# Block inverse of an RWKV-7 scan: every second head's 64x64 products cross to the other half of the partitions

## The chip, the cores and the metric

The kernel runs on one core of a Trainium2 chip. The metric is the device time of one execution in microseconds (us), as the median of several. The engines are TensorE (PE in the profile, its weight loads PEld), VectorE (DVE), ScalarE (ACT), GpSimd (POOL) and SyncE (SP), which here only issues DMAs. Each has its own program and meets the others at semaphores.

## What is computed

One layer of a hybrid block on 2048 tokens of width 1024: RMSNorm, an input projection, a mixer of two groups (8 RWKV-7 heads of width 64 and a spatial gate), an output projection, cross-attention to 256 memory tokens, and a SwiGLU network. The change is in the RWKV-7 heads. Cut to that:

```python
def wkv7_scan(r, w, k, v, kk, a):
    def step(S, inp):
        r_t, w_t, k_t, v_t, kk_t, a_t = inp
        sa = jnp.einsum('bhvk,bhk->bhv', S, -kk_t)
        S = (S * w_t[:, :, None, :]
             + sa[..., None] * (kk_t * a_t)[:, :, None, :]
             + v_t[..., None] * k_t[:, :, None, :])
        y = jnp.einsum('bhvk,bhk->bhv', S, r_t)
        return S, y
```

The kernel does not step through the tokens. It takes them in chunks of 64, where `sa` of a chunk is the solution of a triangular system. So each head and chunk needs the inverse of a unit triangular 64x64 matrix.

## The kernel before

The stage of the heads comes after the input projection and before the output projection. It goes over 16 groups of 128 tokens (`GROUPS`). One group holds 16 triangular matrices: head pair `m` (0 to 3), head `e` of the pair (0 or 1), and `a` (0 or 1), which says on which half of the partitions the matrix lies (`lane(a)`: partitions 0 to 63 or 64 to 127) and which chunk of 64 tokens it is. The inverse `inv` has the shape [128, e, m, 64].

It is built by doubling. It starts as the identity with 2x2 blocks put in (`take_first`), and five levels (`LEVELS` = 2, 4, 8, 16, 32) join neighbouring blocks. A level has these steps, each on another engine than the one before it:

1. PE, `cross` (L1942): 16 products of `inv_t` (the transposed inverse) with the scores `atrb`, 32 columns each, into PSUM.
2. ACT, `evac_x` (L1220): copies PSUM into `xm`.
3. PE, `merge` (L1953): 16 products of `xm` with `inv`, again 32 columns each.
4. DVE, `take_level` (L2551, in the helper `take`): puts the result into `inv` under a mask.
5. DVE, `turned` (L2566): transposes `inv` into `inv_t` for the next level.

Every level is cut in two by the parity `g` of the head pair. The half `g` = 0 goes to bank 0 and `g` = 1 to bank 1, and each half has its own semaphore count at every step. So `cross` of `g` = 1 may run while ACT copies `g` = 0. All 16 products read one half of the partitions and write the same half (`unit(a, g, ...)` from `lane(a)`): of the array's four 64x64 tiles (row half, column half) they use the two on the diagonal.

Each engine has one hand-written order of work, `body`, which mixes three groups: the state and outputs of group k (`state_...`), the inverse and scores of group b = k + 1, and the preparation of group n = k + 2. The order on PE in one body, with the inverse in capitals: from_values, state_out 0, state_in 0, scores of `bt`, solve 0, scores of `kt`, state_add 0, chunk_out 0, CROSS 0, state_out 1, state_in 1, MERGE 0, mix_gate, solve 1, CROSS 1, state_add 1, turn_gate, MERGE 1, chunk_out 1, turn kt, loras, CROSS 2, key_norms, variance, bonus_sums, MERGE 2, lora_g, CROSS 3, turn_v, MERGE 3, key_scales, scale_back, turn bt, CROSS 4, MERGE 4. `turn bt` transposes `bt` into PSUM; ACT copies that into `b_tok`. `solve` of the next body needs the finished inverse.

ACT in one body: identities, rhs_t 0, sa_t 0, inputs, xm 0, rhs_t 1, sa_t 1, xm 1, outputs, k_tok, `lora_tanh` (L1244, tile `th`), xm 2, `roots` (L1252, after a load of the function table), `deviation`, `exps` (after a second load), xm 3, gate, v_tok, b_tok, xm 4.

DVE in one body: take_first, transposes 0, scores into `atrb`, next_state 0 (writes `h_st`, L2593), scores into `qkrm`, take 0, transposes 1, mixed, next_state 1, take 1, transposes 2, gate statistics, `sum_decays` (waits for `th`), `bounded` (waits for ACT's roots), take 2, transposes 3, two reciprocals, `gate_hat`, `bonuses`, take 3, transposes 4, keys_normed, normalised, queries, decayed (writes `bt` of the group after), take 4.

## Time and profile before

| what | us |
|---|---|
| median of 3 runs | 2953.13 (2949.37 to 2953.44) |
| the profiled execution's own time | 2955.44 |
| its span, first to last instruction | 2953.6 |
| the stage of the 16 groups in it, about | 594 to 1040 |

The profile comes from one execution. A row of the grouped views gives a line of the kernel, the engine, what is written and read, shapes and count, then the busy time, the mean of one instruction in ns, and the idle time just before it with what ended it. A row of the timeline gives the start in us, the length in us, engine, line, operation, tiles and count; several like instructions are merged into one row, whose length runs from the first start to the last end. A product of fp32 operands makes two PE records, so 16 products are x32. Instructions in one queue overlap a little: the second of two copies starts before the first has ended.

### The profile page before, as it was taken

The numbers are of one execution on the slowest core, as the hardware profiler recorded it, in microseconds if no ns is written. First come the engines' busy times: TensorE is split into PE (matmuls) and PEld (weight loads), VectorE is DVE, ScalarE is ACT, GpSimd is POOL, SyncE is SP. The second block draws the span as 40 slices with busy tenths as digits, with TensorE's granted clock in tenths as the row PEclk, the third lists the DMA queues.
The fourth block names the chain that finished last, engine by engine and source line by source line (L and its number), as shares of the span: only waits on it lengthen the run. The fifth ranks groups of instructions, "written<-read, shape, count | busy, mean of one in ns | idle before, by whom it ended". The sixth has DMA issues, their size and how long they took to land.

```text
span 2953.6 us, 56334 instructions
## 1 busy us (share of the span) xinstructions
PE 2894.0 (98%) x23722; PEld 2461.5 (83%) x23722; DVE 1590.1 (54%) x2062; ACT 1000.5 (34%) x1740; POOL 1484.9 (50%) x1070
## 2 busy tenths in 40 slices
PE   8999999999999999999999999999999999999998
PEld 7888888888888879987888888787998788888887
DVE  7331633377777632339666644544234966674453
ACT  4122312244554522325333322231333433332222
POOL 4554543456666544276544433556426654553344
PEclk9999999999999999999999999999999999999999
DMA  4533356422232231112333356344111223336632
GB/s 159 186 111 97 122 164 191 148 67 53 57 79 68 66 104 37 51 50 84 111 128 142 122 214 236 134 143 157 43 44 43 100 111 125 142 121 228 228 143 86
DMA packets 175572, 346.56 MB, mean 117 GB/s; under 512 B 46816, under 2 KB 104352, under 8 KB 169696
## 3 DMA queue, kind: packets, MB, share of 16 engines
q1 hardware_dynamic: 175328, 343.06, 34.2%
q8 instruction: 184, 3.01, 0.4%
q14 instruction: 60, 0.49, 0.1%
HBM read 240.24 MB, written 102.76 MB: 116 GB/s over the span
## 4 chain that ended last, share of the span: by engine, by line
PE 48%; DVE 3%; issue 1%; DMA 1%; POOL 1%; ACT 0%; DVEq 0%; SPq 0%; ACTq 0%; POOLq 0%
PE ps L2259 29%; PE ps L1697 14%; PE ps L2211 3%; DMA w_raw<-in_weights 1%; DVE normed L3185 0%; DVE t_raw L2879 0%; POOL sumsq L853 0%; PE ps L2417 0%; DVE t_raw L2887 0%; POOL sq L851 0%; DVE rstd L2429 0%; PE ps L2231 0%; DVE t_lo L2893 0%; POOL w_lo L833 0%; DVE normed L3211 0%
## 5 line engine op out<-in xcount | busy, mean ns | idle before, releaser
L833 POOL TENSOR_TENSOR w_lo<-w_raw,w_hi 128x512 fp32r<-128x512 f32 x232 | 334.9, 1467 | 504.3 <-ACT w_hi L1138 500.6
L1697 PE MATMUL ps<-a_hi,w_hi 128*128 128x512 f32 x1140 | 446.0, 391 | 10.5 <-DVE a_lo L2439 10.0
L1697 PE MATMUL ps<-a_lo,w_hi 128*128 128x512 f32 x1140 | 444.7, 390 | 0.0
L1697 PE MATMUL ps<-a_hi,w_lo 128*128 128x512 f32 x1140 | 351.8, 390 | 0.0
L1138 ACT ACTIVATE w_hi<-w_raw 128x512 fp32r<-128x512 f32 x228 | 129.9, 623 | 623.9 <-PE ps L1697 481.4
L2259 PE MATMUL ps<-a_hi,w_hi 128*128 128x512 f32 x800 | 313.8, 392 | 12.5 <-ACT p_t L1524 4.9
L2259 PE MATMUL ps<-a_lo,w_hi 128*128 128x512 f32 x800 | 312.4, 390 | 0.0
L2259 PE MATMUL ps<-a_hi,w_lo 128*128 128x512 f32 x800 | 312.3, 390 | 0.0
L1697 PEld LDWEIGHTS ps<-a_hi,w_hi 128*128 128x128 f32 x1140 | 214.6, 188 | 55.4 <-DVE a_lo L2439 10.0
L1697 PEld LDWEIGHTS ps<-a_hi,w_lo 128*128 128x128 f32 x1140 | 214.6, 188 | 44.8
L1697 PEld LDWEIGHTS ps<-a_lo,w_hi 128*128 128x128 f32 x1140 | 214.7, 188 | 44.1 <-issue 0.2
L1064 POOL TENSOR_TENSOR w_lo<-w_raw,w_hi 128x512 fp32r<-128x512 f32 x100 | 143.2, 1432 | 182.7 <-ACT w_hi L1508 182.7
L1064 POOL TENSOR_TENSOR w_lo<-s,w_hi 128x512 fp32r<-128x512 f32 x100 | 146.0, 1460 | 163.1 <-ACT w_hi L1508 163.1
L2801 DVE TENSOR_TENSOR x<-ps,x 128x1024 f32 (+1 forms) x63 | 76.7, 1222 | 267.9 <-PE ps L1697 255.2
L2447 DVE TENSOR_TENSOR z_ext<-ps,rstd 128x1024 f32<-128x1024 f32 x44 | 53.9, 1226 | 304.7 <-PE ps L1697 304.2
L1697 PE MATMUL ps<-b_hi,w_hi 128*128 128x512 f32 x512 | 202.3, 395 | 3.7 <-DVE x L2801 3.7
L1697 PE MATMUL ps<-b_lo,w_hi 128*128 128x512 f32 x512 | 200.9, 392 | 0.0
L1064 POOL TENSOR_TENSOR xw_lo<-s,xw_hi 128x512 fp32r<-128x512 f32 x100 | 145.1, 1455 | 110.7 <-ACT xw_hi L1508 110.7
L2259 PE MATMUL ps<-t_hi,xw_hi 128*128 128x512 f32 x496 | 193.5, 390 | 1.3 <-DVE u_t L2949 1.1
L2259 PE MATMUL ps<-t_lo,xw_hi 128*128 128x512 f32 x496 | 193.2, 389 | 0.0
L2259 PE MATMUL ps<-t_hi,xw_lo 128*128 128x512 f32 x496 | 193.0, 389 | 0.0
L2259 PEld LDWEIGHTS ps<-a_hi,w_hi 128*128 128x128 f32 x800 | 150.7, 188 | 47.8 <-ACT p_t L1524 6.6
(381 smaller groups left out, 6392.0 us busy)
## 6 DMA issues: line engine op xcount, KB each, us to landing
w_raw<-in_weights SPq DMA_DIRECT2D x228, 512.0 KB, 4.1
hidden<-hid SPq DMA_DIRECT2D x44, 1024.0 KB, 3.9
zT<-z_out SPq DMA_DIRECT2D x44, 512.0 KB, 3.4
a_hi<-hidden SPq DMA_DIRECT2D x44, 512.0 KB, 8.4
a_lo<-hidden SPq DMA_DIRECT2D x44, 512.0 KB, 9.6
w_raw<-kvw SPq DMA_DIRECT2D x32, 512.0 KB, 3.3
suv<-zT SPq DMA_DIRECT2D x16, 512.0 KB, 4.5
x<-in_xT SPq DMA_DIRECT2D x16, 512.0 KB, 5.7
```

Source lines behind the costliest of these rows:

```text
L833: pool.tensor_tensor(low_t[:, part, :], w_raw[:, u, part, :], high[:, part, :].bitcast(F32), ALU.subtract).then_inc(S["w_lo_done"], 1)
L1064: pool.tensor_tensor(operand(o, p)[1], operand_raw[o], operand(o, p)[0].bitcast(F32), ALU.subtract).then_inc(S["sw_lo"], 1)
L1138: act.activation(split_into(pair, u)[0][:, part, :], w_raw[:, u, part, :], ACT.Copy).then_inc(S["w_hi_done"], 1)
L1697: mm = pe.matmul(to[:, nb, 0:w], wt[:, k, :], r[:, k, nb * w:(nb + 1) * w], start=(k == 0 and r is hi_in and wt is high), stop=(k == kn - ...
L2211: mm = pe.matmul(to, st[:, k, at:at + P], wt[:, 0:2, k, :], start=(k == 0 and n == 0 and t % 2 == 0), stop=(k == KT - 1 and n == 2), skip_ ...
L2259: mm = pe.matmul(to, wt[:, k, :], r[:, k, :], start=(k == 0 and n == 0 and not more), stop=(k == HT - 1 and n == 2), skip_group_check=True)
L2447: dve.tensor_tensor(z_ext[:, u, 1:TB + 1], flat(src), rstd[:], ALU.mult).then_inc(S["job_out"], 1)
L2801: dve.tensor_tensor(at_k(x, k), flat(slot(beside + u)).unsqueeze(1), at_k(x, k), ALU.add).then_inc(S["job_out"], 1)
```

## The change

The cut by parity of the pair (`g`) is replaced by a cut by `e`. Matrices with `e` = 0 go as before. Products of `e` = 1 write the other half of the partitions (`unit(a ^ e, e, ...)`), so `cross` and `merge` now use all four 64x64 tiles. The results of `e` = 1 are thereby on the wrong half, and ACT (`evac_x`) and DVE (`take_level`) bring them back with two copies over 64 partitions each, in place of one over 128. Both waits of `cross` become one wait for both transposes, and both waits of `merge` one wait for all three copies. `xm` is laid out by `e` first, and the transposes read contiguous columns. On PE, `turn bt` goes from before `cross` 4 to between `cross` 4 and `merge` 4.

```diff
-                for g in range(2):
-                    act.wait_ge(S["x_ps"], 10 * n + 2 * lv + g + 1)
-                    act.activation(xm[:, :, g].rearrange("p e m (n two b) -> p e (m n) two b", two=2, b=b)[:, :, :, 0, :],
-                                   ps[:, g, 2 * L:3 * L].rearrange("p (e n b) -> p e n b", e=2, b=b), ACT.Copy).then_inc(S["x_ev"], 1)
+                for e in range(2):
+                    act.wait_ge(S["x_ps"], 10 * n + 2 * lv + e + 1)
+                    for to, frm in crossed(e):
+                        act.activation(sides(xm, e, to, b)[:, :, 0, :], blocks_in(e, 2 * L, frm, b), ACT.Copy).then_inc(S["x_ev"], 1)
...
+        def crossed(e):
+
+            if e == 0:
+                return ((slice(0, P), slice(0, P)),)
+            return ((lane(0), lane(1)), (lane(1), lane(0)))
...
-                for g in range(2):
-                    pe.wait_ge(S["inv_tr"], 10 * n + 2 * lv + g + 1)
-                    for mh, e, a in by_tile():
-                        t_u = inv_t[lane(a), g, 2 * e + mh, :].rearrange("p (n two b) -> p n two b", two=2, b=b)[:, :, 0, :]
-                        mm = pe.matmul(unit(a, g, 2 * L + e * C + mh * 32, 32), atrb[par][lane(a), e, 2 * mh + g, 0, :], t_u,
-                                       start=True, stop=True)
-                    mm.then_inc(S["x_ps"], 1)
+                pe.wait_ge(S["inv_tr"], 10 * n + 2 * lv + 2)
+                for m, e, a in by_tile():
+                    t_u = inv_t[lane(a), e, m, :].rearrange("p (n two b) -> p n two b", two=2, b=b)[:, :, 0, :]
+                    mm = pe.matmul(unit(a ^ e, e, 2 * L + m * 32, 32), atrb[par][lane(a), e, m, 0, :], t_u, start=True, stop=True)
+                    if (m, a) == (HP - 1, 1):
+                        mm.then_inc(S["x_ps"], 1)
...
-                for g in range(2):
-                    pe.wait_ge(S["x_ev"], 10 * n + 2 * lv + g + 1)
...
+                pe.wait_ge(S["x_ev"], 15 * n + 3 * lv + 3)
+                for m, e, a in by_tile():
+                    u_u = inv[par][lane(a), e, m, :].rearrange("p (n two b) -> p n two b", two=2, b=b)[:, :, 1, :]
+                    mm = pe.matmul(unit(a ^ e, e, m * 32, 32), xm[lane(a), e, m, :], u_u, start=True, stop=True)
+                    if (m, a) == (HP - 1, 1):
+                        mm.then_inc(S["tu_ps"], 1)
...
                 if behind:
+                    cross(b, q, 4)
                     turn(b, bt, "bt_done", (S["sg_vh"], min(b + 2, GROUPS)), 3, "btr")
-                    cross(b, q, 4)
                     merge(b, q, 4)
...
-                    dve.wait_ge(S["tu_ev"], 11 * n + (2 * lv + g if lv else 1))
-                    dve.transpose(inv_t[:, g], units(inv[par], g)).then_inc(S["inv_tr"], 1)
+                for e in range(2):
+                    dve.wait_ge(S["tu_ev"], 16 * n + ((3 * lv - 1, 3 * lv + 1)[e] if lv else 1))
+                    dve.transpose(inv_t[:, e], inv[par][:, e]).then_inc(S["inv_tr"], 1)
...
-                for g in range(2):
-                    dve.wait_ge(S["tu_ps"], 10 * n + 2 * lv + g + 1)
-                    take(rights(inv[par], g, b), low[:, lv + 1, 1].rearrange("p (m n b) -> p m n b", m=HP, b=b),
-                         ps[:, g, 0:2 * C].rearrange("p (m n b) -> p m n b", m=HP, b=b), "tu_ev")
+                for e in range(2):
+                    dve.wait_ge(S["tu_ps"], 10 * n + 2 * lv + e + 1)
+                    for to, frm in crossed(e):
+                        take(sides(inv[par], e, to, b)[:, :, 1, :], low[frm, lv + 1, 1].rearrange("p (n b) -> p n b", b=b),
+                             blocks_in(e, 0, frm, b), "tu_ev")
```

The order on the two engines where this matters most follows, at the end of a body. Numbers in names tell apart buffers of one tile; `n_208` is a tile of row scales, `cst` the identity matrix, and the brackets name the semaphores that an instruction waits for. First PE before, from `scale_back` (L1861) to the first product of the next body (L1966):

```order
L1861 MATMUL ps<-n_208,lnr 128x128 [waits gate_done,vtc,yv_rc]
L1861 MATMUL ps<-n_208,lnr 128x128 x3
L1899 MATMUL ps<-cst,bt 128x128 [waits sg_vh,bt_done]
L1899 MATMUL ps<-cst,bt 128x128 x3
L1942 MATMUL ps<-inv_t,atrb_172 64x32 [waits inv_tr]
L1942 MATMUL ps<-inv_t,atrb_172 64x32 x7
L1942 MATMUL ps<-inv_t,atrb_172 64x32 [waits inv_tr]
L1942 MATMUL ps<-inv_t,atrb_172 64x32 x7
L1953 MATMUL ps<-inv_182,xm 64x32 [waits x_ev]
L1953 MATMUL ps<-inv_182,xm 64x32 x7
L1953 MATMUL ps<-inv_182,xm 64x32 [waits x_ev]
L1953 MATMUL ps<-inv_182,xm 64x32 x7
```

And the same place with the change, where these lines are L1865, L1903, L1945 and L1955:

```order
L1865 MATMUL ps<-n_208,lnr 128x128 [waits gate_done,vtc,yv_rc]
L1865 MATMUL ps<-n_208,lnr 128x128 x3
L1945 MATMUL ps<-inv_t,atrb_172 64x32 [waits inv_tr]
L1945 MATMUL ps<-inv_t,atrb_172 64x32 x15
L1903 MATMUL ps<-cst,bt 128x128 [waits sg_vh,bt_done]
L1903 MATMUL ps<-cst,bt 128x128 x3
L1955 MATMUL ps<-inv_182,xm 64x32 [waits x_ev]
L1955 MATMUL ps<-inv_182,xm 64x32 x15
```

Two waits of eight products each have become one of sixteen, and the transposes of `bt` now stand between the two. On ACT the end of the body, with the change:

```order
L1306 ACTIVATE gate_188<-ps 128x512 [waits lg_ps]
L1282 ACTIVATE v_tok_173<-ps 128x512 [waits vtr]
L1282 ACTIVATE b_tok_175<-ps 128x512 [waits btr]
L1225 ACTIVATE xm<-ps 128x4x32 [waits x_ps]
L1225 ACTIVATE xm<-ps 64x4x32 [waits x_ps]
L1225 ACTIVATE xm<-ps 64x4x32
L1241 ACTIVATE inv_187<-half_id 128x512
```

The copy into `b_tok`, which waits for `turn bt`, stood before the `xm` copies of level 4 already and still does; the `xm` copies were two over 128 partitions. On DVE one level (take 3 and the transposes for 4) with the change:

```order
L2651 TENSOR_TENSOR bon_raw<-zin_157,ps 128x512 [waits bon_ps]
L2554 COPY_PREDICATED inv_182<-low,ps 128x8x16 [waits tu_ps]
L2554 COPY_PREDICATED inv_182<-low,ps 64x8x16 [waits tu_ps]
L2554 COPY_PREDICATED inv_182<-low,ps 64x8x16
L2569 STREAM_TRANSPOSE inv_t<-inv_182 128x256 [waits tu_ev] x2
L2657 TENSOR_TENSOR kk<-zin_158,ps 128x512 [waits kb_ps]
```

Before, two masked copies of 128x4x2x16 stood there. In the whole program ACT and DVE get 80 instructions more each (16 groups by 5 levels), PE as many as before.

## Rows read from the trace of the kernel before

**Rows 1.** The page, busy time of each engine over the whole span

```profile
PE 2894.0 (98%) x23722; PEld 2461.5 (83%) x23722; DVE 1590.1 (54%) x2062; ACT 1000.5 (34%) x1740; POOL 1484.9 (50%) x1070
```

**Rows 2.** Stretches: length, busy us by engine, PE clock, DMA share, GB/s

```profile
615.60:1028.20 412.60, 401.18 (x11008) 357.03 (x11005) 302.29 (x665) 207.24 (x485) 260.90 (x249) 1.00 0.25 65
...
1030.00:1040.00 10.00, 5.48 (x162) 4.81 (x160) 6.21 (x5) 7.28 (x12) 5.14 (x4) 0.77 0.49 134
```

**Rows 3.** Waits from 620 to 1020 us: total, times, longest

```profile
POOL v_ln L978 <- DVE bt L2670: 33.5, 14, 2.4
...
PE ps L1942 <- DVE atrb L2551: 4.8, 8, 0.7
```

**Rows 4.** Groups by line on PE: busy us, mean ns, idle before

```profile
L1953 PE MATMUL ps<-inv,xm 64*64 64x32 f32 x2560 | 89.9, 220 | 0.3 <-issue 0.3
```

**Rows 5.** Timeline of PE, one group from body start to body start

```profile
809.33 1.13 PE L1966 MATMUL ps<-v_tok,qkrm 64*64 64x64 f32 x32
...
811.87 0.57 PE L2005 MATMUL ps<-rhs_t,inv 64*64 64x64 f32 x14
...
814.95 1.12 PE L1942 MATMUL ps<-inv_t,atrb 64*64 64x32 f32 x32 [0.65 <-DVE atrb L2551]
815.91 0.51 PE L1987 MATMUL ps<-qr,h_st 64*64 64x64 f32 x10
...
824.94 1.12 PE L1942 MATMUL ps<-inv_t,atrb 64*64 64x32 f32 x32
...
829.76 1.12 PE L1942 MATMUL ps<-inv_t,atrb 64*64 64x32 f32 x32
830.81 1.16 PE L1910 MATMUL ps<-cent,zin 128*128 128x128 f32 x8
831.90 1.12 PE L1953 MATMUL ps<-inv,xm 64*64 64x32 f32 x32
...
834.04 0.66 PE L1899 MATMUL ps<-cst,bt 128*128 128x128 f32 x4
834.63 1.12 PE L1942 MATMUL ps<-inv_t,atrb 64*64 64x32 f32 x32
835.66 1.12 PE L1953 MATMUL ps<-inv,xm 64*64 64x32 f32 x32
836.62 1.13 PE L1966 MATMUL ps<-v_tok,qkrm 64*64 64x64 f32 x32
```

**Rows 6.** Timeline of PE, products of `chunk_out`, which use all four tiles

```profile
1033.28 0.41 PE L2029 MATMUL ps<-qkrm,v_tok 64*64 64x64 f32 x16
1033.51 0.41 PE L2029 MATMUL ps<-atrb,sa_t 64*64 64x64 f32 x16
```

**Rows 7.** Timeline of DVE in the same group

```profile
815.23 0.54 DVE L2593 TENSOR_TENSOR h_st<-h,w_end 128x256 f32<-128x256 f32 x1
...
828.60 0.48 DVE L2551 COPY_PREDICATED inv<-low,ps 128x128 f32<-128x128 uint8 x2
828.99 0.76 DVE L2566 STREAM_TRANSPOSE inv_t<-inv 128x256 f32<-128x256 f32 x2
...
832.60 0.30 DVE L2551 COPY_PREDICATED inv<-low,ps 128x128 f32<-128x128 uint8 x1
833.07 0.30 DVE L2551 COPY_PREDICATED inv<-low,ps 128x128 f32<-128x128 uint8 x1 [0.17 <-PE ps L1953]
833.27 0.76 DVE L2566 STREAM_TRANSPOSE inv_t<-inv 128x256 f32<-128x256 f32 x2
```

**Rows 8.** Timeline of ACT in the same group

```profile
825.05 1.02 ACT L1244 ACTIVATE th<-ps 128x1024 f32<-128x1024 f32 x1 [0.51 <-PE ps L1818]
825.98 0.44 ACT L1220 ACTIVATE xm<-ps 128x128 f32<-128x128 f32 x2
...
834.74 0.60 ACT L1278 ACTIVATE b_tok<-ps 128x512 f32<-128x512 f32 x1 [2.12 <-PE ps L1899]
835.33 0.28 ACT L1220 ACTIVATE xm<-ps 128x128 f32<-128x128 f32 x1
```

More of the change, by code:

```diff
@@ L270, in hybrid_block_kernel @@
         n8 = rw("n8", [P, 4, L])
-        xm = rw("xm", [P, 2, 2, 2, C])
+        xm = rw("xm", [P, 2, HP, C])
         rhs_t = rw("rhs_t", [P, 2, 2, RN])
@@ L480, in side, with sides, blocks_in @@
             return j ^ (m // 2)
-        def units(t, g):
-            first = t[:, 0, g]
-            return bass.AP(first.tensor, first.offset, [[2 * HP * C, P], [2 * C, HP], [1, C]])
-        def rights(t, g, b):
-            first = t[:, 0, g]
-            return bass.AP(first.tensor, first.offset + b, [[2 * HP * C, P], [2 * C, HP], [2 * b, C // (2 * b)], [1, b]])
+        def sides(t, e, part, b):
+            return t[part, e].rearrange("p m (n two b) -> p (m n) two b", two=2, b=b)
+        def blocks_in(bank, at, part, b):
+            return ps[part, bank, at:at + L].rearrange("p (n b) -> p n b", b=b)
+        def crossed(e):
+            if e == 0:
+                return ((slice(0, P), slice(0, P)),)
+            return ((lane(0), lane(1)), (lane(1), lane(0)))
         def bank4(b):
@@ L1920, in scores @@
                 elif n:
-                    pe.wait_ge(S["tu_ev"], 11 * n)
+                    pe.wait_ge(S["tu_ev"], 16 * n)
                 for m in range(HP):
@@ L1929, in by_tile @@
             def by_tile():
-                return [(mh, e, a) for mh in range(2) for e in range(2) for a in range(2)]
+                return [(m, e, a) for m in range(HP) for e in range(2) for a in range(2)]
             def cross(n, par, lv):
@@ L1937, in cross @@
                     pe.wait_ge(S["ev_b"], 2 * n + 2)
-                for g in range(2):
-                    pe.wait_ge(S["inv_tr"], 10 * n + 2 * lv + g + 1)
-                    for mh, e, a in by_tile():
-                        t_u = inv_t[lane(a), g, 2 * e + mh, :].rearrange("p (n two b) -> p n two b", two=2, b=b)[:, :, 0, :]
-                        mm = pe.matmul(unit(a, g, 2 * L + e * C + mh * 32, 32), atrb[par][lane(a), e, 2 * mh + g, 0, :], t_u,
-                                       start=True, stop=True)
-                    mm.then_inc(S["x_ps"], 1)
+                pe.wait_ge(S["inv_tr"], 10 * n + 2 * lv + 2)
[4 more added lines that the diff above has]
+                        mm.then_inc(S["x_ps"], 1)
             def merge(n, par, lv):
                 b = LEVELS[lv]
-                for g in range(2):
-                    pe.wait_ge(S["x_ev"], 10 * n + 2 * lv + g + 1)
-                    for mh, e, a in by_tile():
-                        u_u = inv[par][lane(a), e, 2 * mh + g, :].rearrange("p (n two b) -> p n two b", two=2, b=b)[:, :, 1, :]
-                        mm = pe.matmul(unit(a, g, e * C + mh * 32, 32), xm[lane(a), e, g, mh, :], u_u, start=True, stop=True)
-                    mm.then_inc(S["tu_ps"], 1)
+                pe.wait_ge(S["x_ev"], 15 * n + 3 * lv + 3)
[4 more added lines that the diff above has]
+                        mm.then_inc(S["tu_ps"], 1)
             def from_values(k, par):
@@ L2002, in solve @@
                 if j == 0:
-                    pe.wait_ge(S["tu_ev"], 11 * k + 11)
+                    pe.wait_ge(S["tu_ev"], 16 * k + 16)
                 for m, e, a in by_pair(j):
@@ L2577, in take_level @@
                 b = LEVELS[lv]
-                for g in range(2):
-                    dve.wait_ge(S["tu_ps"], 10 * n + 2 * lv + g + 1)
-                    take(rights(inv[par], g, b), low[:, lv + 1, 1].rearrange("p (m n b) -> p m n b", m=HP, b=b),
-                         ps[:, g, 0:2 * C].rearrange("p (m n b) -> p m n b", m=HP, b=b), "tu_ev")
+                for e in range(2):
[3 more added lines that the diff above has]
+                             blocks_in(e, 0, frm, b), "tu_ev")
                 if lv + 1 < len(LEVELS):
```

## Prediction

> **What bounds the kernel now.** The page comes first: PE is busy for 98% of the span, DVE for 54%, POOL for 50%, ACT for 34% [rows 1]. So a gain has to come from PE's time, unless PE only looks busy. The stretch that holds the change is read next. From the first body's start at 615.60 us to the last one's end at 1028.20 lie 15 bodies, 27.5 us each, with PE busy for 401.18 of 412.60 us and DVE for 302.29, which is 73% and far above its mean over the span [rows 2]. PE's waits there are few: the one that names another engine's work is for `atrb`, 4.8 us in 8 times [rows 3]. One body, 809.33 to 836.62, takes 27.29 us and shows it once, 0.65 us before `cross` 0 [rows 5]. So PE's own issue sets the pace in this stage, and the other engines have slack, but little on DVE.
>
> **What a block of products costs.** `cross` 4 starts at 834.63, `merge` 4 at 835.66, the next body at 836.62 [rows 5]. A block of 16 products lasts 1.12 us, of which 0.22 is the run of its last product [rows 4], so it issues for 0.90, and the queue is held 0.96 to 1.03 with the passage to the next block. That is 0.06 us for each pair of product records, on two tiles. `chunk_out` shows four tiles: its two halves of 16 records start 0.23 us apart [rows 6], 0.46 for 32 records. Those products have 64 columns, ours 32, so width doesn't favour them. I take 0.46 for a changed block, 0.47 less than now. Ten blocks in a body would be 4.7 us, 70 us over 15 bodies, if nothing else bound.
>
> It is not so. The body has to be cut where PE meets the others, at ACT's `th` (825.05 [rows 8]), which starts as soon as `loras` is through. Before it lie 15.72 us with four blocks, behind it 11.57 us with six.
>
> **First half.** Four blocks save 4 x 0.47 = 1.88 us. But `cross` 0 starts when DVE's `atrb` is there, which the change doesn't move, and what follows it, `state_out` 1, needs `h_st`, which ends at 815.23 + 0.54 = 815.77; now `state_out` starts at 815.91 [rows 5, 7]. So of the first 0.47 only about 0.1 is kept. The half becomes 15.72 - 1.88 + 0.4 = 14.24 us. The copies of levels 0 and 1 lie under `state_out`, `state_in`, `state_add`, `turn_gate`, `mix_gate` and `solve` 1, which PE does meanwhile, so I cost them at nothing; without that cover each level would show some 0.35 us.
>
> **What the added copies cost.** The trace has no copy over 64 partitions between halves. The nearest rows are the 128-partition copies of as many elements per partition. On ACT two take 0.44 us, one 0.28, so the second adds 0.16; on DVE two take 0.48, one 0.30, so it adds 0.18 to 0.19 [rows 7, 8]. Bounds: nothing below half of that, as each still is an instruction; above, the full 0.28 and 0.30 if copies that cross halves don't overlap. I take 0.16 and 0.19, since lanes work side by side.
>
> **Second half, from the start of `th`.** DVE ends the transposes 3 at 828.99 + 0.76 = 829.75, th + 4.70 [rows 7]. The change puts one ACT copy ahead of the roots for which DVE waits, and one DVE copy: th + 5.05. PE reaches `cross` 3 after 829.76 - 824.94 = 4.82 us, less 0.94 for two blocks, that is at th + 3.8 [rows 5]. So PE waits some 1.3 us there: **DVE takes over as the bound.** From transposes 3 to transposes 4 DVE needs 834.03 - 829.75 = 4.28 us; a copy adds 0.19, and the waits between the halves of take 3 (832.60 to 833.07, where 0.19 would do [rows 7]) give back 0.28: th + 9.25. `merge` 3 is early enough: 5.1 + 0.46 + 1.2 for `turn_v` [rows 5] and the copies of level 3, and it is through before th + 7.8, when DVE wants it.
>
> Then the move of `turn bt` counts. `cross` 4 at th + 9.3 holds PE 0.58, the transposes of `bt` end 0.66 later, th + 10.53 [rows 5]. ACT's `b_tok` stands ahead of `xm` in its queue and waits for them. It holds ACT 0.5 to 0.6 (834.74 to 835.33 [rows 8]), and behind it the three copies need 0.16 + 0.16 + 0.28 = 0.60: th + 11.7. `merge` 4 starts there, 0.5 later the next body: th + 12.2, against 11.57 now. So six cheaper blocks make this half 0.6 us **longer**. Before, `b_tok` was fed ahead of `cross` 4 and cost nothing.
>
> Behind `merge` 4 the take of level 4 ends by th + 13.0, while `solve` 0 comes 2.5 us into the body (811.87 after 809.33 [rows 5]), at th + 14.7. POOL's 2.4 us wait for `bt` in a body [rows 3] says that its queue has room. No DMA is moved, and PE's count of products stays.
>
> **Sum.** 14.24 + 12.2 = 26.44 us against 27.29: -0.85 a body, -12.8 over 15. The blocks ahead of the first body (594 to 615.6) give perhaps another 1. Against the profiled execution's own 2955.44 us that is 2941.6; its like from the median 2953.13 is 2939.5.
>
> **Two rules of the Trainium skill.** The products of one block all go to bank `e`, from both row halves at once. Today's pairs of diagonal tiles share a bank too, while the four-tile `chunk_out` gives each row half a bank of its own, and its pace is twice theirs [rows 5, 6]. Four tiles on shared banks have no row. "TensorEngine Tiling (Array Packing)", section "Restrictions and Gotchas", says that different row tiles cannot access the same PSUM bank at one time. By it the blocks would gain nothing, and the time would be that of rival B; no row here shows it at work or not. The same page under "Performance Considerations" warns that tiling speeds up TensorE but not the evacuation of PSUM. The trace agrees: with PE alone the sum was 70 us above, with the copies counted it is 13.
>
> **Rivals.**
> A, copies at full length. If a copy between halves overlaps with none, levels 2 and 3 add 0.4 us more on DVE and ACT each and level 4 another 0.24: 0.85 a body is lost again, and the time is 2953 or a little above. Against: pairs overlap everywhere [rows 7, 8].
> B, tiles don't overlap; **slower**. Blocks stay at 0.93. The first half is 15.8. In the second, `merge` 3 ends at th + 8.4 instead of 7.8, `cross` 4 and `merge` 4 give 0.47 each behind transposes, so 12.2 becomes 13.6: 29.4 a body, +2.1, and 2985 us. It decides from the point where a block takes over about 0.65 us. For: the shared banks, and that no row has this mix. Against: two row halves write one bank today, and a tile still makes a record every 0.06 us (32 records on two tiles in 0.9), as in `chunk_out` (32 on four in 0.46), so nothing slows a tile for sharing its bank [rows 5, 6].
> C, the clock falls; slower. From 1030 to 1040 us PE is busy 5.48 of 10 us and the granted clock is 0.77, a mix of 1.2 and 2.4 GHz; with PE busy 97% it stays at 1.00 [rows 2]. After the change PE would be busy about 83%, its longest wait 1.3 us. At half clock for a part of each body it costs 1 us or more a body: 2960 to 2975.
> D, DVE has more room than I think (shorter transposes from contiguous columns, copies that add less than 0.1). Then a body keeps up to 2 us: 2920 to 2930.
> E, nothing binds but PE: 2885.
>
> **How the numbers follow.** Forecast 0.58 (2930 to 2947), A 0.13, B 0.09, C 0.06, D 0.11, E 0.03. The range 2924 to 2956 takes in the forecast, A, and most of D. Within 0.2% means within 5.9 us, about what a measurement of this kernel can tell; a few of the forecast's cases and all of A end there or near. Faster by more 0.70, within 0.14, slower by more 0.16.
>
> **What would show it.** Blocks L1945 and L1955 of 0.65 to 0.70 us per 32 records instead of 1.12; groups of about 26.5 us; three `xm` copies in about 0.6 us, three takes in about 0.7; waits of PE of over 1 us before `cross` 3 (for `inv_t`) and before `merge` 4 (for `xm`), behind a `b_tok` that waits for L1903; a new wait of 0.4 us before `state_out` 1. Wrong if blocks keep 1.12 us (B), if the clock falls under 1.00 in the stage (C), or if `cross` 3 doesn't wait (D or E).

## The result and the profile after

The changed kernel takes 3002.65 us (median of 4 runs, 3001.71 to 3003.66) against 2952.78 for the kernel before on the same chip: the ratio is 1.0165, 95% interval 1.0144 to 1.0187. It is **slower by 50 us**, where 2939.5 was forecast, and it lies outside the range.

The page after, busy time by engine and the granted clock in 40 slices of the span:

```profile
PE 2874.8 (96%) x23722; PEld 2431.5 (81%) x23722; DVE 1627.5 (54%) x2142; ACT 1030.4 (34%) x1820; POOL 1485.7 (50%) x1070
...
PEclk9999999988989889999999999999999999999999
```

PE has the same 23722 records as before [rows 1] and is busy 19 us less, while the span grew by 46.3 us (2953.6 to 2999.9). Digits of 8 stand in the clock only where the changed stage lies. The stage itself, the same 15 bodies, in the view of stretches, and ahead of it the blocks before the first body (length; busy us and records of PE, PEld, DVE, ACT, POOL; clock; DMA share; GB/s):

```profile
620.53:1077.99 457.46, 385.21 (x11008) 331.59 (x11006) 339.73 (x739) 233.42 (x560) 260.00 (x248) 0.90 0.22 59
...
594.00:620.53 26.53, 20.23 (x413) 15.52 (x413) 16.54 (x36) 14.30 (x32) 15.03 (x15) 0.84 0.22 65
```

In [rows 2] the stage took 412.60 us at a clock of 1.00. Now a body takes 30.50 us instead of 27.51, and the clock's mean over the stage is 0.90. PE's busy time fell by 16.0 us although a part of it ran at half clock. The account of the span: 15 bodies of 2.99 us more are 44.9; the first body starts 4.9 us later; what follows the last one is 3.5 us shorter. That is 46.3.

One body on PE, in its second half (start us, length us, engine, line, operation, tiles, shapes, count, and in brackets the idle time before with what ended it); `cross` is L1945, `merge` L1955, `turn bt` L1903, `turn_v` L1914, the next body begins with L1969:

```profile
825.84 0.67 PE L1945 MATMUL ps<-inv_t,atrb 64*64 64x32 f32 x32 [1.58 <-DVE inv_t L2569]
826.44 1.62 PE L1914 MATMUL ps<-cent,zin 128*128 128x128 f32 x8
828.00 1.08 PE L1955 MATMUL ps<-inv,xm 64*64 64x32 f32 x32
...
830.92 0.67 PE L1945 MATMUL ps<-inv_t,atrb 64*64 64x32 f32 x32
831.52 0.66 PE L1903 MATMUL ps<-cst,bt 128*128 128x128 f32 x4
833.62 0.98 PE L1955 MATMUL ps<-inv,xm 64*64 64x32 f32 x32 [1.45 <-ACT xm L1225]
834.38 1.96 PE L1969 MATMUL ps<-v_tok,qkrm 64*64 64x64 f32 x32
```

Three things answer to [rows 5]. A block is 0.67 us long where it was 1.12. PE waits 1.58 us before `cross` 3 and 1.45 us before `merge` 4; before, it waited at neither. And what follows each wait is slow: `turn_v` takes 1.62 us where it took 1.16, `merge` 3 takes 1.08 for the same 32 records that take 0.67 elsewhere, `from_values` 1.96 for 1.13. The stretches of just this time, cut close to where the granted clock changes (826.97, 830.38, 833.80 and 837.21 us):

```profile
824.50:827.10 2.60, 1.26 (x37) 1.22 (x38) 2.54 (x6) 2.56 (x6) 2.33 (x3) 0.97 0.03 6
827.13:830.54 3.41, 3.41 (x53) 3.12 (x51) 2.87 (x8) 1.52 (x4) 2.74 (x3) 0.52 0.00 0
830.54:833.96 3.42, 1.86 (x59) 1.39 (x58) 2.81 (x5) 1.68 (x5) 0.47 (x1) 0.98 0.00 0
833.98:837.39 3.41, 3.41 (x94) 3.41 (x94) 0.90 (x3) 0.24 (x1) 3.27 (x3) 0.53 0.02 5
837.40:845.00 7.60, 6.57 (x273) 6.13 (x267) 6.15 (x12) 3.03 (x9) 5.01 (x6) 1.00 0.37 94
```

PE is busy for 1.26 of 2.60 us, and behind it the clock is 0.52, which is the level of 1.2 GHz but for the edges of the stretch; then it comes back to 2.4, PE is busy for 1.86 of 3.42 us, and it falls to 0.53 again. In the slow stretches PE is busy all the time. Summed over the 15 bodies, 95.6 us ran at the low level. The two waits stand in nearly every body (1.58 and 1.45 us, the first missing in the last body), and most of them have a low stretch behind them, but not all: there is none in the first body.

On the two copying engines (same columns), DVE in this half and ACT at `th` and at the end of the body:

```profile
824.07 0.91 DVE L2554 COPY_PREDICATED inv<-low,ps 128x128 f32<-128x128 uint8 x3
825.02 0.77 DVE L2569 STREAM_TRANSPOSE inv_t<-inv 128x256 f32<-128x256 f32 x2
```

```profile
820.40 1.02 ACT L1248 ACTIVATE th<-ps 128x1024 f32<-128x1024 f32 x1 [0.48 <-PE ps L1822]
821.32 0.86 ACT L1225 ACTIVATE xm<-ps 128x128 f32<-128x128 f32 x3
...
832.21 0.60 ACT L1282 ACTIVATE b_tok<-ps 128x512 f32<-128x512 f32 x1 [3.51 <-PE ps L1903]
832.70 0.87 ACT L1225 ACTIVATE xm<-ps 128x128 f32<-128x128 f32 x3
```

The row's shape is that of its first copy; the other two are over 64 partitions. Three takes last 0.91 us (two lasted 0.48 [rows 7]), three `xm` copies 0.86 (two lasted 0.44 [rows 8]). So each added copy costs 0.43 us, not 0.16 or 0.19. And `merge` 4 stands behind `b_tok`, which waits for the moved `turn bt`: 831.52, 832.21, 832.70, 833.62. The waits of PE from 620 to 1020 us (total, times, longest):

```profile
PE ps L1945 <- DVE inv_t L2569: 26.6, 31, 1.6
PE ps L1955 <- ACT xm L1225: 18.8, 13, 1.5
PE ps L1945 <- DVE atrb L2554: 6.2, 12, 0.7
PE ps L1990 <- DVE h_st L2597: 4.6, 13, 0.5
```

In what follows a body is cut at ACT's `th`, as in the prediction. The means over 14 bodies:

| | first half | second half | low clock in the 15 bodies |
|---|---|---|---|
| before | 16.09 | 11.56 | 0 |
| after | 16.62 | 14.03 | 95.6 us |

### The profile page after: what moved, and what is told of

Same layout as the page of the kernel before. It is cut to its first block and busy times, and to the rows that moved or that the text cites. A ratio compares the mean times of both kernels' runs of the same rounds, so it can differ in the third digit from the quotient of the medians.

```text
span 2999.9 us, 56494 instructions
## 1 busy us (share of the span) xinstructions
PE 2874.8 (96%) x23722; PEld 2431.5 (81%) x23722; DVE 1627.5 (54%) x2142; ACT 1030.4 (34%) x1820; POOL 1485.7 (50%) x1070
```

## The experiments

Four theories stood for the 3 us of a body: added copies that don't overlap (rival A), a falling clock (rival C), the move of `turn bt`, and tiles that hinder each other on a shared bank (rival B). All ratios are to the kernel before, on the same chip, with a 95% interval.

**The move undone in the changed kernel (e1).**

```diff
                 if behind:
-                    cross(b, q, 4)
                     turn(b, bt, "bt_done", (S["sg_vh"], min(b + 2, GROUPS)), 3, "btr")
+                    cross(b, q, 4)
                     merge(b, q, 4)
```

> The changed kernel with one thing undone: the transposes of bt stand ahead of cross 4 again, so b_tok no longer holds up the xm copies of level 4. Clock theory (each of two PE waits of over 1.4 us in a body is followed by a stretch at half clock): the wait before merge 4 shrinks to under 1 us, one of the two low stretches in a body goes, and the body loses 0.8 us of wait and about 1.7 us of slow products: about 2965 us, mean granted clock up from 0.978 to about 0.986. Queue theory (only the waits count, the clock costs little): 0.8 us a body, about 2990 us.

Measured: 2979.68 us, ratio 1.0084 (1.0067 to 1.0101). That gives back 23 of the 50 us, 1.30 us in a body, with 69.4 us left at the low clock; 2965 had been expected, with one of the two low stretches gone. The waits don't fix the clock alone: the wait before `cross` 3 is 1.57 us in every body but the last, and yet three bodies in a row (858 to 942 us) have no low stretch. In e1 PE still waits before `merge` 4, 1.0 us at most, now for `xm` alone.

**The move alone in the kernel before (e5).** The same swap, made the other way round, in the old kernel.

> The kernel before with one thing of the change: the transposes of bt go behind cross 4. Queue theory: ACT's b_tok then waits for them ahead of the xm copies of level 4, and merge 4 comes later by cross 4, the transposes and b_tok less what PE did before, about 0.9 us a body, so the second half of a body grows from 11.56 to about 12.5 us and the time to about 2966 us. If the move is harmless and only the copies and the clock count: within 5 us of 2952.

Measured: 2970.79 us, ratio 1.0076 (1.0059 to 1.0093). The stage of e5, then PE and ACT at the end of a body of e5:

```profile
615.89:1044.19 428.30, 404.09 (x11010) 358.57 (x11008) 307.51 (x665) 203.87 (x485) 259.57 (x249) 1.00 0.24 63
```

```profile
816.00 1.12 PE L1953 MATMUL ps<-inv,xm 64*64 64x32 f32 x32 [0.85 <-ACT xm L1220]
```

```profile
815.18 0.60 ACT L1278 ACTIVATE b_tok<-ps 128x512 f32<-128x512 f32 x1 [3.17 <-PE ps L1899]
```

The second half of a body is 12.51 us instead of 11.56: **the move costs 0.95 us a body by itself**, with nothing else changed and a clock of 1.00 in the mean of the stage. `b_tok` holds up `xm`, as the prediction's chain had it.

**Work for PE in its waits (e2).** The changed kernel with products whose results nobody reads: six more of `lora_g` ahead of `cross` 3, six of the identity behind `turn bt`.

```diff
+                low_rank(gl, gd[par], 7)
+                for m in range(2):
+                    pe.matmul(cols(7, m), gl[:, m * P:(m + 1) * P], gd[par][:, 0:L], start=True, stop=True)
...
+            def fill(count):
+                for _ in range(count):
+                    pe.matmul(cols(2, 0), ident, ident, start=True, stop=True)
...
                     turn(b, bt, "bt_done", (S["sg_vh"], min(b + 2, GROUPS)), 3, "btr")
+                    fill(6)
                     merge(b, q, 4)
```

> The changed kernel with products added that change nothing: six more products (records of 0.11 us each) ahead of the last ones of lora_g, before the wait of cross 3, and six of the identity with itself into a free bank between the transposes of bt and merge 4. They do no useful work and only keep PE busy while it waited. Clock theory: the granted clock stays at 1.00 in the stage, the low stretches go, and the time falls by 30 to 45 us to 2955 to 2970. Queue theory: the waits are only filled, the time stays at 3000 us or rises by a few us.

Measured: 2982.72 us, ratio 1.0111 (1.0086 to 1.0136). The stage of e2:

```profile
620.15:1055.50 435.35, 386.64 (x11378) 333.70 (x11371) 340.71 (x739) 232.46 (x561) 260.46 (x249) 1.00 0.24 62
```

The clock is 1.00 through the stage, no time at the low level is left, and with 370 more records PE has a shorter stage: 29.02 us a body instead of 30.50. So the falling clock comes with PE's idle time in these waits and goes when they are filled, and it costs about 1.5 us a body. The expectation wanted more: 1.5 us a body over the kernel before remain at full clock.

**The move undone and the fillers (e9).** e1 with six and four such products.

> The changed kernel with the transposes of bt ahead of cross 4 again and useless products added in two waits: six ahead of the last ones of lora_g, four of the identity between cross 4 and merge 4. Clock and queue theories together: no stretch at half clock in the stage, the second half of a body at 12.2 us, the first at 15.5, body 27.8 us: about 2960 us; what is left to 2952 is what the copies cost beyond what four tiles save. If the two effects don't add: 2975 us or more.

Measured: 2966.69 us, ratio 1.0056 (1.0039 to 1.0073), a body of 28.20 us, 3.4 us at the low clock:

```profile
620.83:1043.86 423.03, 383.64 (x11320) 329.60 (x11314) 337.20 (x739) 233.82 (x561) 261.49 (x249) 1.00 0.24 63
```

Without the move and all but without the low clock the changed kernel is still 0.7 us a body slower than before. That rest is neither of the two, and it lies in the second half: 12.19 us as expected (12.2), against 11.56 before. The first half is 16.08, as before, where 15.5 had been expected.

**Whole copies (e3).** Both copies of `e` = 1 are replaced by one straight copy over 128 partitions on each engine. The tiles stay; the second heads' results are not brought back.

```diff
-                    for to, frm in crossed(e):
-                        act.activation(sides(xm, e, to, b)[:, :, 0, :], blocks_in(e, 2 * L, frm, b), ACT.Copy).then_inc(S["x_ev"], 1)
+                    act.activation(sides(xm, e, slice(0, P), b)[:, :, 0, :], blocks_in(e, 2 * L, slice(0, P), b), ACT.Copy).then_inc(S["x_ev"], 1 + e)
```

and the same in DVE's takes.

> The changed kernel with all four tiles, but the results of e = 1 are copied straight, in one copy of 128 partitions on ACT and on DVE, and so stay on the wrong half: the swap of the halves is left out. Copies theory (a copy of 64 partitions costs its full 0.30 and 0.33 us, two of them 0.4 us more on each engine and level than one): DVE and ACT take back about 0.9 us before cross 3, 0.4 before cross 4 and 0.4 before merge 4, 1.7 us a body, 25 us, to 2975 us, and to about 2940 if the shorter waits also keep the clock up. If the copies don't matter: within 5 us of 3000.

Measured: 2952.19 us, ratio 0.9998 (0.9989 to 1.0008). The stage:

```profile
614.14:1023.21 409.07, 347.12 (x11018) 296.33 (x11010) 303.87 (x664) 201.25 (x486) 260.72 (x249) 0.99 0.25 65
```

The time lies between the 2975 and the 2940 that were expected. The whole 50 us hang on the copies that bring the second heads back: with as many copies as before, all over 128 partitions, the second half is 11.33 us, although `turn bt` still stands behind `cross` 4. Against e2, which has the same order and tiles and no low clock, that is 1.85 us less: the price of bringing the second heads back on ACT and DVE. Since PE waits less in e3, the clock stays up without fillers (10.2 us at the low level). That e3 isn't faster than before is the move of `turn bt` once more: undone here too (e12, below), it gives back 0.60 us in the second half, less than the 0.95 of e5.

**Four tiles or two (e4).** The changed kernel with its products on the diagonal tiles again and three copies per level that stay within their half.

```diff
-            return ((lane(0), lane(1)), (lane(1), lane(0)))
+            return ((lane(0), lane(0)), (lane(1), lane(1)))
...
-                    mm = pe.matmul(unit(a ^ e, e, 2 * L + m * 32, 32), atrb[par][lane(a), e, m, 0, :], t_u, start=True, stop=True)
+                    mm = pe.matmul(unit(a, e, 2 * L + m * 32, 32), atrb[par][lane(a), e, m, 0, :], t_u, start=True, stop=True)
```

and the same in `merge`.

> The changed kernel with everything kept (three copies a level, one wait for both halves, the moved transposes of bt) but the products on the two diagonal tiles again, so the copies of e = 1 stay within their half. Clock theory: blocks take 0.93 us again, PE is busy for longer, the clock stays near 1.00, and a body takes about 29.5 to 30 us: 2985 to 2995 us, no slower than the changed kernel. If four tiles were worth their 0.47 us a block in spite of the clock: 30 us slower than the changed kernel, 3030 us.

Measured: 3046.91 us, ratio 1.0310 (1.0290 to 1.0331), above what was expected. The stage and the blocks ahead of it:

```profile
630.27:1126.12 495.85, 446.04 (x11008) 393.79 (x11006) 341.61 (x739) 225.62 (x560) 257.97 (x248) 0.91 0.21 55
...
594.00:630.27 36.27, 33.13 (x409) 27.09 (x409) 16.76 (x36) 13.98 (x32) 15.46 (x15) 0.60 0.17 48
```

A body is 33.06 us, 2.6 more than with four tiles. The clock fell here too, which the expectation had excluded, so the size isn't clean. The sign is: PE is busy for 446.04 us where four tiles need 385.21, and the clock is 0.91 in one and 0.90 in the other. With the blocks of 0.67 us above, rival B is out.

**Two copies instead of one in the kernel before (e8).** Tiles and order as before; the copies of the second heads are split into two over 64 partitions, straight.

```diff
-                    act.activation(xm[:, :, g].rearrange("p e m (n two b) -> p e (m n) two b", two=2, b=b)[:, :, :, 0, :],
-                                   ps[:, g, 2 * L:3 * L].rearrange("p (e n b) -> p e n b", e=2, b=b), ACT.Copy).then_inc(S["x_ev"], 1)
+                    for a in (slice(0, P),) if g == 0 else (lane(0), lane(1)):
+                        act.activation(xm[a, :, g].rearrange("p e m (n two b) -> p e (m n) two b", two=2, b=b)[:, :, :, 0, :],
+                                       ps[a, g, 2 * L:3 * L].rearrange("p (e n b) -> p e n b", e=2, b=b), ACT.Copy).then_inc(S["x_ev"], 1)
```

and the same in DVE's takes.

> The kernel before with one thing of the change: the second half (g = 1) of every level is copied by two copies of 64 partitions each, on ACT and on DVE, within their own half of the partitions; tiles, waits and the place of the transposes stay. Copies theory: each extra copy costs its engine 0.30 us on ACT and 0.33 on DVE; in the second half of a body DVE has no slack for three of its own and one of ACT's, so the body grows by 0.9 to 1.2 us and the time to 2966 to 2970 us. If copies hurt only where they cross the halves: under 2957.

Measured: 2963.78 us against 2950.22 on this chip, ratio 1.0051 (1.0035 to 1.0068). Only 0.48 us a body, about half of what was expected, in the second half (12.04 for 11.56). The profiled execution is 14.9 us longer than that of the kernel before, and the bodies make up 7.2 of them: the first one starts 11.7 us later, behind a stretch at half clock like the one in the next experiment, and what follows the last is 4 us shorter. The copies, three in a row, straight on DVE in e8 and on ACT in e4:

```profile
820.90 0.82 DVE L2552 COPY_PREDICATED inv<-low,ps 128x128 f32<-128x128 uint8 x3
```

```profile
816.26 0.73 ACT L1225 ACTIVATE xm<-ps 128x128 f32<-128x128 f32 x3
```

0.82 and 0.73 us, where crossing takes 0.91 and 0.86. So of the 0.43 us that two half copies cost above a whole one, 0.34 on DVE and 0.29 on ACT come without crossing. The starts in the traces (medians over the bodies), a copy alone being 0.30 long on DVE and 0.27 on ACT: from one 128-partition copy to the next 0.19 (DVE) and 0.16 us (ACT); from a 128-partition copy to a straight one of the lower half 0.20 and 0.16; from there to the upper half 0.32 and 0.29; in the changed kernel each step is 0.30 to 0.33. That half a copy is no cheaper than a whole one stands in the groups by line of the changed kernel (busy us, mean ns, idle before):

```profile
L2554 DVE COPY_PREDICATED inv<-low,ps 64x128 f32<-64x128 uint8 x160 | 51.8, 324 | 5.2 <-PE ps L1955 0.2
L1225 ACT ACTIVATE xm<-ps 64x128 f32<-64x128 f32 x160 | 43.9, 275 | 3.9
```

So a copy overlaps with the one before only where both start on the same partitions; a copy that differs from its forerunner in what it reads alone (the first crossing one) is held back already. One that differs in what it writes alone isn't among them. Each crossing copy starts elsewhere than its forerunner and waits until that one is done. For DVE the Trainium skill has this as a rule, in "VectorE: DVE Perf Modes", section "Two Vector instructions with no wait between them": "A held instruction starts only when every earlier Vector instruction has finished", and by the model given there one is held when an input starts in another group of 32 partitions than the last read of that memory, or its output in another than the last write to it. The trace agrees in each case above. ACT's copies, for which only the rows speak, behave alike.

**The swap where it is covered (e6, e10, e11).** e6 has four tiles, crossing copies and joint waits on levels 0 and 1 alone; levels 2 to 4 go on diagonal tiles with two whole copies, each `e` with its own wait, and `turn bt` stands ahead again.

```diff
+        CROSSED = 2
...
-            if e == 0:
+            if e == 0 or lv >= CROSSED:
...
-                pe.wait_ge(S["inv_tr"], 10 * n + 2 * lv + 2)
-                for m, e, a in by_tile():
+                for m, e, a in by_tile(lv):
+                    if (m, a) == (0, 0):
+                        pe.wait_ge(S["inv_tr"], 10 * n + 2 * lv + (2 if lv < CROSSED else e + 1))
```

> The change kept for levels 0 and 1 alone, the levels in the first half of a body; levels 2 to 4 go on the two diagonal tiles with one copy for each e and a wait for each e, and the transposes of bt stand ahead of cross 4. Copies theory: the first half of a body falls from 16.1 to 15.4 us, the second stays at 11.6, no wait of PE is over 1 us, the clock stays at 1.00: about 2943 us. Rival (four tiles bring nothing wherever they are, since the first half is held by copies and by the supply of instructions): within 4 us of 2952.

Measured: 2958.79 us, ratio 1.0031 (1.0020 to 1.0043). The stage and what is ahead of it:

```profile
626.40:1034.75 408.35, 382.48 (x11007) 334.13 (x11004) 318.23 (x694) 215.51 (x515) 259.05 (x248) 1.00 0.25 66
...
594.00:626.40 32.40, 29.93 (x409) 24.22 (x409) 16.12 (x35) 13.47 (x29) 15.62 (x15) 0.63 0.18 54
```

The bodies gained less than expected, 27.22 us for 27.51: the first half fell from 16.09 to 15.76 us, where 15.4 had been expected. The gain was lost before them: from 594 us to the first body PE is busy for 29.93 of 32.40 us at a clock of 0.63; the kernel before needs 21.60 us for that. So e10 is e6 with group 0, whose blocks lie there, left as before, and e11 is e10 with level 0 alone. The edit of e10 against e6:

```diff
         CROSSED = 2
+        def far(n, lv):
+
+            return n > 0 and lv < CROSSED
```

> e6 with the first group (n = 0, whose levels run ahead of the first body) on two tiles with whole copies, as in the kernel before; groups 1 to 15 have four tiles on levels 0 and 1. In e6 a body took 27.22 us against 27.51, but the blocks ahead of the first body, with 27 us at half clock, took 11 us more. If that stretch came from the copies of the first group, it goes: first body at 615.6 us again, the time 4 to 5 us under that of before, 2945 to 2947. Rival (the bodies bring their own low stretches as soon as the first is gone, or the 0.3 us were chance): 2950 or more.

> e10 with four tiles on level 0 alone. Waits theory: what cross 0 saves is spent before state_out 1, which waits for h_st, and what merge 0 saves is spent before cross 1 behind three takes instead of two: the first half of a body within 0.2 us of 16.1, the time within 3 us of before. If the copies are cheap here: as far below before as e10 or further.

Measured: e10 2949.88 us against 2952.92, ratio 0.9987 (0.9978 to 0.9995); e11 2952.01 us, ratio 0.9993 (0.9984 to 1.0001). e10's stage starts at 614.41 and has a clock of 1.00; a body is 27.36, and the 2945 to 2947 us that were expected are missed: the stretch at half clock is gone, as foreseen, but half of the gain in the bodies went too. e10 is the best kernel here that leaves nothing out, and its gain of 3 us is at the edge of what can be told. e11 can't be told from no change in its time; its bodies take 27.27 us, no more than those of e10, so the second level on four tiles shows no gain of its own.

**What would remain if the swap were free (e12).** e3 with `turn bt` ahead of `cross` 4 again.

> Four tiles at all levels, whole copies that leave the results of e = 1 on the wrong half (the swap of the halves is left out), and the transposes of bt ahead of cross 4: what four tiles would give if nothing had to be brought back. The queue theory takes 1.0 us off the second half of e3, to 10.3 us; with the first half at 16.1 a body is 26.4 us and the time about 2937 us if the clock holds, 2950 if the shorter PE work brings stretches at half clock.

Measured: 2936.58 us, ratio 0.9941 (0.9929 to 0.9953), the time as expected, though a body is 26.73 us instead of 26.4. The stage of the profiled execution, which with 2942.85 us was the longest of the six:

```profile
617.12:1018.11 400.99, 345.14 (x11017) 293.75 (x11010) 297.94 (x665) 202.73 (x486) 260.54 (x248) 1.00 0.26 67
```

The halves of a body, at full clock: the second 10.73 for 11.56, the first 16.17 for 16.09. So even with nothing to bring back and no clock lost, four tiles on all ten blocks are worth 16 us, not 70, and nothing of it is in the first half, where four blocks save 1.9 us of PE's issue. Taken together, PE's waits for nothing that the profile shows ("issue") are the largest there; two of their rows, from 620 to 1020 us of e12:

```profile
PEld ps L1944 <- issue: 8.9, 24, 1.5
...
PE ps L1944 <- issue: 5.0, 7, 1.4
```

In the kernel before, such waits sum to 5.8 us on PE and 36.1 on PEld; in e12 to 24.0 and 59.4. In the first half of a body they are 1.52 us in e12 and 0.31 in the kernel before; the wait for `h_st`, which the prediction foresaw, is another 0.40. That looks like instructions that come late. The queue `q8 instruction` on the profile's page may be what brings them: in the trace of before it moves 88 pieces of 16 KB during the stage, one for every 250 of PE's 22013 records there. In the body that starts at 836.62 they start at 837.48, 841.24, 845.06 and 848.92, 3.8 us apart, and then at 854.64, 860.78 and 864.97. Among the pieces that start in the first 12 us of a body the median distance is 3.8 us before, 3.9 in e12 and 3.9 in e13 (below), whatever PE has to do there; the shortest is 3.3 to 3.4.

**More records in the first half (e13).** e12 with the products of `cross` 0 and `cross` 1 issued twice, 128 more instructions in a half where PE has the room for them if only other engines bind it.

```diff
-                for m, e, a in by_tile():
+                for last, (m, e, a) in [(r, t) for r in ((0, 1) if lv < 2 else (1,)) for t in by_tile()]:
...
-                    if (m, a) == (HP - 1, 1):
+                    if last and (m, a) == (HP - 1, 1):
```

> e12 with the 16 products of cross 0 and of cross 1 issued twice, which changes no value and adds 64 product records and 64 weight loads to the first half of a body. In e12 the first half took 16.17 us on average and 14.63 in its best body, and PE stood still for 0.5 to 1.5 us at changing places where no engine was late. Supply theory (the first half is bound by how fast instructions come to PE, 16 KB or 256 instructions in no less than 3.8 us, 15 ns each): 128 more instructions add 1.9 us, the first half is 18.0 us, the time 28 us above e12. Rival (the stalls have another cause and only PE's own time counts, 0.46 us a block, of which cross 0's is hidden before state_out 1): 0.5 to 0.9 us more, 16.7 to 17.1 us, at most 14 us above e12.

Measured: 2969.75 us, ratio 1.0057 (1.0040 to 1.0074). The stage:

```profile
614.45:1043.94 429.49, 365.18 (x12014) 312.51 (x12011) 298.91 (x668) 202.73 (x486) 261.82 (x249) 0.99 0.24 63
```

The first half went from 16.17 to 17.93 us, the second stayed at 10.73. 128 instructions cost 1.76 us (1.60 without the two bodies that hold a stretch at the low clock); at 3.8 us for 250 they would cost 1.9. PE's own issue of the same records, two blocks on four tiles, would be 0.9 us, and only where nothing covered it. The time is 33 us above e12, where 28 had been expected for this theory and 14 at most for the rival. The doubled blocks themselves show the two paces: 18 of 30 issue their 64 records in 0.90 to 1.04 us, which is PE's own pace, and 12 stand still on the way and take 1.34 to 2.33. **The first half of e12 is bound by how fast PE gets its instructions**, and a product that is issued in half the time is still one instruction. The link to the queue itself stays an inference: the cost per instruction fits, the waits are there, but no run changed the supply.

## Why the prediction was wrong

The second half of the body above against the prediction, counted from the start of `th` (820.40):

| | predicted | after |
|---|---|---|
| `cross` 3 | 5.1 | 5.44 |
| `cross` 4 | 9.3 | 10.52 |
| `merge` 4 | 11.7 | 13.22 |
| next body | 12.2 | 13.98 |

On the mean of the 14 bodies, the second half grew by 2.47 us: +0.95 for the moved `turn bt` (e5), -1.18 for four tiles and joint waits (e3 against e5), +1.85 for the copies that cross (e2 against e3), +0.85 for the clock (after against e2). The steps are differences between kernels, so what one hides of another is counted in the later one; e2's fillers could also take a little where a wait has grown shorter than they are. The order matters: without the move, four tiles and joint waits are worth -0.83 (e12 against before) and the move then 0.60 (e3 against e12). No run separates four tiles from the joint waits.

The sum forecast -1.48 us for the first half and +0.63 for the second; the runs show +0.53 and +2.47. Of the 3.85 us a body that it missed, 1.60 are the clock (e2), 1.26 the first half at full clock (15.87 in e2 against 16.09), and 0.99 the second half at full clock (13.18 in e2), above all the copies. So the sum had three errors of like size, and they are taken in the order in which they arise.

- **A block of 16 products, 0.46 for 0.93: right.** Nearly all of them run 0.65 to 0.71 us per 32 records at full clock, with 0.45 from the first start to the last. Tiles of different rows write one bank at one time without loss, each on its own half of the partitions (`unit(a ^ e, e, ...)`: in bank `e` the two row halves never write the same half). So in this form rival B and the rule behind it ("Restrictions and Gotchas" of "TensorEngine Tiling (Array Packing)" in the Trainium skill) are not borne out: four tiles on a shared bank go at the pace that [rows 6] show for separate ones.
- **Added copies, 0.16 and 0.19: mis-sized; this step failed first.** They cost 0.43 per level and engine against two whole copies: 0.30 to 0.33 for the third, and the second no longer overlaps either. In the second half the sum counted four of them on the path: 0.16 and 0.19 ahead of `cross` 3, 0.19 ahead of `cross` 4, 0.16 ahead of `merge` 4, together 0.70. Four times 0.43 is 1.7, and the runs show 1.85. With 1.0 us more the forecast 12.2 is 13.2, and e2, at full clock, has 13.18. The upper bound, 0.28 and 0.30, was put down as rival A, with a chance of 0.13, because pairs overlap everywhere in [rows 7, 8]. Those pairs start on the same partitions, and the new ones don't.
- **The two waits: right in place, their consequence was not drawn.** 1.3 us were forecast before `cross` 3 and 1.58 came; the wait for `xm` behind `b_tok` came as 1.45, and the chain through `turn bt` was priced nearly right. But behind most of these waits of 1.5 us the clock fell, and with the waits filled it didn't (e2). Rival C had this with a chance of 0.06 and "1 us or more a body"; it cost some 1.5. The row it drew on, 5.48 of 10 us busy at 0.77 [rows 2], was the nearest to what came: around the waits PE is busy for 1.26 of 2.60 and 1.86 of 3.42 us. I looked at the mean over a body instead, 83%, which hides them.
- **A and C were weighed as alternatives, and came together.** Longer copies make the waits longer, and longer waits lower the clock. A's price of 2953 assumed full clock, C's of 2960 to 2975 assumed short copies.
- **First half, 14.24 us: wrong.** The shortest of the 14 is 15.19, and with the clock up (e2) the mean is 15.87 for 16.09 before. The starting point was low as well: the body of [rows 5] has the shortest first half of the 14, 15.72 us. Two terms were put at nothing. The copies weren't free: the wait for `inv_t` before `cross` 1 is 0.35 us in the mean, and that for `h_st`, forecast as 0.4, is 0.37. And the sum had no term for the pace at which PE gets its instructions. Where copies cost nothing more than before (e12), that pace takes most of the gain: the waits for "issue" grow from 0.31 to 1.52 us. In e2 they are 0.65, beside 0.28 for `inv_t` and 0.44 for `h_st`, so there both errors count. In the changed kernel itself they are 0.17, and the low clock costs 0.75 us in this half. "PE's own issue sets the pace", drawn from [rows 2, 3], mixed two things: PE busy, and PE supplied.
- **Ahead of the first body, -1 us: wrong,** +4.9, with 8.4 us at the low clock.
- **"So six cheaper blocks make this half longer": right in sign,** and the sum of both halves then took its sign from the first, which gave nothing.

The two waits just named, on PE in the first half of the same body of the changed kernel (it starts at 805.21, so this is the half of 15.19 us):

```profile
811.76 0.51 PE L1990 MATMUL ps<-qr,h_st 64*64 64x64 f32 x10 [0.26 <-DVE h_st L2597]
...
815.46 0.67 PE L1945 MATMUL ps<-inv_t,atrb 64*64 64x32 f32 x32 [0.39 <-DVE inv_t L2569]
```

0.26 us stand before `state_out` 1, for `h_st`, and 0.39 before `cross` 1, for transposes that come late by the third take.

Left open: which rule holds ScalarE's copies back; and why in e4, e6 and e8 the clock stays low for 27 to 34 us on end up to the first body and a little into it, while PE is busy over 90% of the time (29.93 of 32.40 us in e6), and why the same wait has a low stretch behind it in one body of e1 and not in the next. Not tried: fewer instructions for PE in the first half, which by e13 should shorten it, and the cut with separate waits on four tiles.

## What to carry to other kernels

Price a copy over half the partitions at its full length unless it starts, reading and writing, where the one before it started, and that holds for the second of two half copies even when nothing crosses; the overlap that a trace shows for like copies isn't there for others. Whenever a change makes PE faster between fixed points, add up the waits it creates, and price the case that the clock falls behind them together with the case that made them long: they aren't alternatives. Read the starting point of a sum from the mean over the bodies, not from one of them. And before counting saved issue time, look at the waits for "issue" and at the number of instructions: products that run in half the time are still as many instructions.

## What the runs showed of the hardware

- Four row and column tiles of 64 by 64 with 32 columns, both row halves writing one bank on different halves of its partitions, issue 32 fp32 records in 0.45 us; two diagonal tiles need 0.90 to 0.93.
- A 64-partition copy of 128 elements lasts 0.275 us on ACT and 0.324 on DVE, about as one over 128 partitions, and overlaps with its forerunner only where both start on the same partitions: 0.16 and 0.20 us from start to start, else 0.29 and 0.33.
- Behind waits of 1.58 and 1.45 us, PE ran at 0.52 and 0.53 of the full clock; behind a like wait of 1.57 us it stayed at full clock in three bodies of e1; and products without use in the waits kept the clock at 1.00 (e2): 370 records more, 22 us less.
- 128 instructions more on PE in a stretch of 16.2 us cost 1.76 us, 14 ns each; where nothing holds them up, 128 such instructions (64 records of products and 64 weight loads) issue in 0.90 us, 7 ns each.
